# Spreading the scan decays of a state-space layer by one matmul of three rounded parts, and rounding the opening weight block earlier in the norms

## The reference

```
def _sublayer(x, fn, mod_j, g, b, weight):
    y = fn(x * (1 + scale) + shift)
    return _layernorm(DEEPNORM_ALPHA * x + weight * gate * y, g, b)

def step(state, inp):                     # the scan of the one state-space mixer
    acum = jnp.cumsum(dtc * a_g, axis=1)
    seg = acum[:, :, None] - acum[:, None, :]
    decay = jnp.exp(jnp.where(causal, seg, -jnp.inf))
    cb = jnp.einsum('blgn,bsgn->blsg', cc, bc)
    y = jnp.einsum('blsg,blsgh,bsghp->blghp', cb, decay, xc * dtc[..., None])
```

## Time and profile before

| | |
|---|---|
| time, median of 3 runs | 3048.01 us (3044.29 to 3054.64) |
| the profiled execution | 3059.89 us, its span 3058.1 us |
| PE busy | 91% of the span |
| DVE, ACT, POOL busy | 64%, 41%, 47% |
| granted TensorE clock, mean over the span | 0.918 |

### The profile page before, as it was taken

How to read it: one execution, slowest core, us unless ns; L and a number is a source line. 1 busy time by engine, 2 the same in 40 slices (tenths; PEclk the granted TensorE clock), 3 DMA queues, 4 the chain that set the end, 5 groups by cost and what they waited for, 6 DMA issues and landing times.

```text
span 3058.1 us, 49684 instructions
## 1 busy us (share of the span) xinstructions
PE 2769.6 (91%) x20691; PEld 2623.7 (86%) x20691; DVE 1963.1 (64%) x2277; ACT 1248.5 (41%) x1386; POOL 1449.5 (47%) x1134
## 2 busy tenths in 40 slices
PE   3998789999984999999989899999878999879999
PEld 3997689999983899999974899899768998679998
DVE  6656866576558765756676675765776555684654
ACT  2434444444433444444442443444434433344443
POOL 0890949659385396692970089298190000000000
PEclk7998889999996999999985899999889998889999
DMA  7775557667562576674740377486553643234453
GB/s 272 258 257 160 178 167 268 233 202 259 193 224 86 181 264 222 216 261 170 263 159 1 131 233 260 157 280 232 166 181 128 223 167 124 70 97 138 152 178 124
DMA packets 357446, 576.23 MB, mean 188 GB/s; under 512 B 22271, under 2 KB 297914, under 8 KB 357178
## 3 DMA queue, kind: packets, MB, share of 16 engines
q1 hardware_dynamic: 357306, 574.29, 55.6%
HBM read 573.20 MB, written 1.05 MB: 188 GB/s over the span
## 4 chain that ended last, share of the span: by engine, by line
PE 72%; DVE 12%; POOL 7%; ACT 3%; issue 3%; DMA 2%; SPq 1%; POOLq 0%; DVEq 0%; ACTq 0%
PE ps L1771 59%; POOL mod_acc L657 4%; PE ps L1824 3%; DVE wlo L1084 2%; POOL mod_w L652 2%; PE ps L2154 2%; ACT whi L695 1%; PE ps L1830 1%; PE ps L2145 1%; PE ps L1881 1%; DMA raw<-in_ffn_w_in_dram 1%; DVE z L1237 1%; DVE z L1215 1%; DMA mod_w<-in_w_mod_dram 1%; DVE conv L1514 1%
## 5 line engine op out<-in xcount | busy, mean ns | idle before, releaser
L1084 DVE TENSOR_TENSOR wlo<-raw,whi 128x2048 fp32r<-128x2048 f32 x387 | 982.4, 2541 | 620.7 <-ACT whi L695 618.9
L1771 PE MATMUL ps<-H_hi,whi 128*128 128x256 f32 x3840 | 1099.7, 286 | 47.1 <-issue 17.5
L1771 PE MATMUL ps<-H_lo,whi 128*128 128x256 f32 x3840 | 1093.5, 285 | 0.0
L1771 PE MATMUL ps<-H_hi,wlo 128*128 128x256 f32 x3840 | 1093.1, 285 | 0.0
L695 ACT ACTIVATE whi<-raw 128x2048 fp32r<-128x2048 f32 (+1 forms) x402 | 760.0, 1892 | 648.8 <-DMA raw<-in_ffn_w_in_dram 259.6
L1771 PEld LDWEIGHTS ps<-H_hi,whi 128*128 128x128 f32 x3840 | 744.3, 194 | 55.6 <-issue 45.8
L657 POOL TENSOR_TENSOR mod_acc<-mod_acc,mod_w 128x512 f32<-128x512 f32 x450 | 790.4, 1784 | 0.0
L1771 PEld LDWEIGHTS ps<-H_lo,whi 128*128 128x128 f32 x3840 | 744.5, 194 | 1.2 <-issue 1.0
L1771 PEld LDWEIGHTS ps<-H_hi,wlo 128*128 128x128 f32 x3840 | 744.2, 194 | 0.0
L1771 PE MATMUL ps<-A_hi,whi 128*128 (+1 forms) x1880 | 537.1, 286 | 21.5 <-DVE wlo L1084 21.5
L1771 PE MATMUL ps<-A_hi,wlo 128*128 (+1 forms) x1880 | 534.6, 284 | 0.0
(11 more groups left out here) (339 smaller groups left out, 2931.7 us busy)
## 6 DMA issues: line engine op xcount, KB each, us to landing
raw<-in_ffn_w_in_dram SPq DMA_DIRECT2D x176, 1024.0 KB, 5.3
mod_w<-in_w_mod_dram SPq DMA_DIRECT2D x180, 768.0 KB, 5.0
raw<-in_ffn_w_out_dram SPq DMA_DIRECT2D x88, 1024.0 KB, 5.0
raw<-in_w_gate_up_dram SPq DMA_DIRECT2D x22, 1024.0 KB, 5.1
raw<-in_ssm_w_in_dram SPq DMA_DIRECT2D x20, 1024.0 KB, 7.3
raw<-in_w_in_dram SPq DMA_DIRECT2D x14, 1024.0 KB, 5.1
raw<-in_diff_w_in_dram SPq DMA_DIRECT2D x12, 1024.0 KB, 8.1
raw<-in_w_down_dram SPq DMA_DIRECT2D x11, 1024.0 KB, 4.9
```

The source lines that it names most:

```text
L1084: tt(wlo[b % RAW][:, r], raw[b % RAW][:, r], whi[b % RAW][:, r].bitcast(F32), ALU.subtract).then_inc(w_lo, 1)
L1771: m = pe.matmul(out, l, r, start=first and i == 0, stop=last and i == 2, skip_group_check=rest)
```

## The change

Two edits. In the scan, the running sums are split into three parts (`ac_hi`, `ac_mid`, `ac_rest`), the three stand negated in 96 partitions of `acT` (now fp32r and 384 columns wide, with the second query half twice), and one fp32r matmul with `threefold` (three stacked unit matrices) adds them up again for head h. Ahead of it into the same bank goes an fp32r matmul of `mask` (1e30 above the diagonal) with `unit`, into the two diagonal blocks. ACT takes the exponential straight from that bank, with `dts[:, 7]` as bias and the scale -1, in two instructions. DVE's `decay` is gone. In the `ln` norms ACT rounds the second weight block before its square 2 and not before its square 4, and DVE takes its first half before `gated(2)` and not before `gated(4)`; `ln_last` stays as it was.

```
 # ACT, act_ln
-                    if c == 4:
+                    if c == (2 if st.kind == "ln" else 4):
                         convert(g.b + g.n + 1)
 # ACT, act_ssm
-                copy(acT[:, :], ps[0:SSM_H, 4, 0:S]).then_inc(s["acum_t"], 1)
+                copy(ac_hi[:, :], ps[0:3 * SSM_H, 4, 0:S]).then_inc(s["part_hi"], 1)
+                nc.scalar.activation(dts[:, 7], ps[:, 5, 0:64].rearrange("p (t h) -> p t h", t=2), ACT.Copy, scale=-1.0)
+                for i in range(3):
+                    r = slice(SSM_H * i, SSM_H * i + SSM_H)
+                    copy(threefold[r, :], ident[r, r])
+                act.wait_ge(s["rest_1"], n["rest_1"] + 1)
+                copy(ac_mid[:, :], ac_rest[:, :]).then_inc(s["part_mid"], 1)
...
+                act.wait_ge(s["rest_2"], n["rest_2"] + 1)
+                for i, x in enumerate((ac_hi[:, :].bitcast(F32), ac_mid[:, :].bitcast(F32), ac_rest[:, :])):
+                    r = slice(SSM_H * i, SSM_H * i + SSM_H)
+                    nc.scalar.activation(acT[r, 0:S], x[r, :], ACT.Copy, scale=-1.0)
+                    i = nc.scalar.activation(acT[r, S:CW], x[r, P:S], ACT.Copy, scale=-1.0)
+                i.then_inc(s["acum_t"], 1)
+                act.wait_ge(s["acum_t"], n["acum_t"] + 1)
                 for h in range(SSM_H):
-                    act.wait_ge(s["dec"], n["dec"] + h + 1)
-                    nc.scalar.activation(dec[:, h % 2, :], dec[:, h % 2, :], ACT.Exp).then_inc(s["dec_exp"], 1)
+                    act.wait_ge(s["spread"], n["spread"] + h + 1)
+                    if h >= 2:
+                        act.wait_ge(s["mixing"], n["mixing"] + h - 1)
+                    for t, (a, b) in enumerate(((0, S), (S, CW))):
+                        i = nc.scalar.activation(dec[:, h % 2, a:b], ps[:, 4 + h % 2, a:b], ACT.Exp, bias=dts[:, 7, t, h:h + 1], scale=-1.0)
+                    i.then_inc(s["dec_exp"], 1)
 # DVE, dve_ln
                 gated(0), gated(1), zsum(1), sqsum(1)
+                if st.kind == "ln":
+                    convert_open(st, 0)
                 gated(2), gated(3), zsum(2), zsum(3), sqsum(2), sqsum(3)
-                convert_open(st, 0)
+                if st.kind == "ln_last":
+                    convert_open(st, 0)
 # DVE, dve_ssm
+                dve.wait_ge(s["part_hi"], n["part_hi"] + 1)
+                tt(ac_rest[:, :], ps[0:3 * SSM_H, 4, 0:S], ac_hi[:, :].bitcast(F32), ALU.subtract).then_inc(s["rest_1"], 1)
...
+                tt(ac_rest[:, :], ac_rest[:, :], ac_mid[:, :].bitcast(F32), ALU.subtract).then_inc(s["rest_2"], 1)
...
-                    ts(dec[:, h % 2, 0:S], src, dts[:, 7, 0, h:h + 1], 0.0, ALU.subtract, ALU.min)
-                    ts(dec[:, h % 2, S:CW], src[:, P:S], dts[:, 7, 1, h:h + 1], 0.0, ALU.subtract, ALU.min).then_inc(s["dec"], 1)
 # PE, pe_ssm
                     if h >= 2:
-                        pe.wait_ge(s["dec"], n["dec"] + h - 1)
-                    pe.matmul(ps[:, 4 + h % 2, 0:S], ident[0:SSM_H, h:h + 1].to_broadcast([SSM_H, P]), acT[:, :], start=True, stop=True)\
+                        pe.wait_ge(s["dec_exp"], n["dec_exp"] + h - 1)
+                    to = ps[:, 4 + h % 2, 0:CW]
+                    pe.matmul(to.rearrange("p (j n) -> p j n", j=3)[:, 0:3:2, :], mask[:, :], unit[:, :].unsqueeze(1).to_broadcast([P, 2, P]),
+                              start=True, stop=False, skip_group_check=True)
+                    pe.matmul(to, threefold[:, h:h + 1].to_broadcast([3 * SSM_H, P]), acT[:, :], start=False, stop=True, skip_group_check=True)\
                         .then_inc(s["spread"], 1)
```

More of the change, by code:

```diff
@@ L172 @@
     "diff": dict(fin_sq=4, fin_sum=4, fin_std=4, fin_n=4, fin_hi=4, fin_lo=4, **{k: 8 for k in ATT}),
-    "ssm": dict(tap=24, conv_out=12, x_turned=8, x_out=8, dt_in=1, dt_ln=1, adt=1, acum=1, acum_t=1, cb=4, cb_out=4, spread=SSM_H,
-                dec=SSM_H, dec_exp=SSM_H, mixing=SSM_H, ssd=SSM_H, y_out=SSM_H // 2,
+    "ssm": dict(tap=24, conv_out=12, x_turned=8, x_out=8, dt_in=1, dt_ln=1, adt=1, acum=1, part_hi=1, rest_1=1, part_mid=1, rest_2=1, acum_t=1,
+                cb=4, cb_out=4, spread=SSM_H, dec_exp=SSM_H, mixing=SSM_H, ssd=SSM_H, y_out=SSM_H // 2,
                 fin_sq=4, fin_sum=4, fin_std=4, fin_n=4, fin_hi=4, fin_lo=4),
@@ L404, in program @@
         pick = at("pick", [P, 11], room(44), F32R)
+        unit, mask = at("unit", [P, P], room(4 * P), F32R), at("mask", [P, P], room(4 * P), F32R)
         std = at("std", [P, 2, S], room(8 * S))
@@ L451, in program @@
         dts = at("dts", [P, 8, 2, SSM_H], o_hf + 16 * S)
-        acT = at("acT", [SSM_H, S], o_hf + 16 * S + 4 * 512)
+        acT = at("acT", [3 * SSM_H, CW], o_hf + 16 * S + 4 * 512, F32R)
+        threefold = at("threefold", [3 * SSM_H, SSM_H], room(4 * SSM_H), F32R)
+        ac_hi, ac_rest = at("ac_hi", [3 * SSM_H, S], o_hl + 16 * CW, F32R), at("ac_rest", [3 * SSM_H, S], o_hl + 16 * CW + 4 * S)
+        a3 = at("a3", [P, 2, 3, SSM_H], o_hh + 16 * CW + 4 * S)
+        ac_mid = at("ac_mid", [3 * SSM_H, S], o_hh + 16 * CW, F32R)
         sqg = at("sqg", [P, 2, 4, S], o_hf)
@@ L766, in act_init @@
                 nc.scalar.activation(tiny[:, 6:8], tiny[:, 4:6], ACT.Exp).then_inc(s["lam_exp"], 1)
+                copy(unit[:, :], ident)
+                nc.scalar.activation(mask[:, :], kc("causal", 0, P), ACT.Copy, scale=-1.0)
                 copy(pick[:, :], kc("pick")).then_inc(s["picked"], 1)
@@ L963, in act_ssm @@
                 act.wait_ge(s["acum"], n["acum"] + 1)
-                copy(acT[:, :], ps[0:SSM_H, 4, 0:S]).then_inc(s["acum_t"], 1)
-                for h in range(SSM_H):
-                    act.wait_ge(s["dec"], n["dec"] + h + 1)
-                    nc.scalar.activation(dec[:, h % 2, :], dec[:, h % 2, :], ACT.Exp).then_inc(s["dec_exp"], 1)
+                copy(ac_hi[:, :], ps[0:3 * SSM_H, 4, 0:S]).then_inc(s["part_hi"], 1)
[5 more added lines that the diff above has]
+                copy(ac_mid[:, :], ac_rest[:, :]).then_inc(s["part_mid"], 1)
+                act.wait_ge(s["part_hi"], n["part_hi"] + 1)
+                act.wait_ge(s["part_mid"], n["part_mid"] + 1)
+                act.wait_ge(s["rest_2"], n["rest_2"] + 1)
[5 more added lines that the diff above has]
+                act.wait_ge(s["acum_t"], n["acum_t"] + 1)
+                for h in range(SSM_H):
+                    act.wait_ge(s["spread"], n["spread"] + h + 1)
[4 more added lines that the diff above has]
+                    i.then_inc(s["dec_exp"], 1)
                 act.wait_ge(s["y_out"], n["y_out"] + 16)
@@ L1531, in dve_ssm @@
                 link(tt(dts[:, 5], dts[:, 4], dts[:, 3], ALU.add))
-                stt(dts[:, 6], dts[:, 5], -1.0, alog[:, :].unsqueeze(1).to_broadcast([P, 2, SSM_H]), ALU.mult, ALU.mult).then_inc(s["adt"], 1)
-                dve.wait_ge(s["acum"], n["acum"] + 1)
-                link(nc.vector.tensor_copy(dts[:, 7], ps[:, 5, 0:64].rearrange("p (t h) -> p t h", t=2)))
+                for i in range(3):
+                    k = stt(a3[:, :, i, :], dts[:, 5], -1.0, alog[:, :].unsqueeze(1).to_broadcast([P, 2, SSM_H]), ALU.mult, ALU.mult)
+                k.then_inc(s["adt"], 1)
+                dve.wait_ge(s["part_hi"], n["part_hi"] + 1)
+                tt(ac_rest[:, :], ps[0:3 * SSM_H, 4, 0:S], ac_hi[:, :].bitcast(F32), ALU.subtract).then_inc(s["rest_1"], 1)
+                dve.wait_ge(s["rest_1"], n["rest_1"] + 1)
+                dve.wait_ge(s["part_mid"], n["part_mid"] + 1)
+                tt(ac_rest[:, :], ac_rest[:, :], ac_mid[:, :].bitcast(F32), ALU.subtract).then_inc(s["rest_2"], 1)
                 for i in range(SSM_G):
@@ L1563, in dve_ssm @@
                 for i in range(SSM_H + 3):
-                    if i < SSM_H:
-                        decay(i)
                     if 1 <= i <= SSM_H:
@@ L2127, in pe_ssm @@
                 pe.wait_ge(s["x_out"], n["x_out"] + 8)
[L2128 to L2131, removed]
+                a0, a1 = a3[:, 0, 0, :], a3[:, 1, 0, :]
+                a0s, a1s = (a3[:, t].rearrange("p c h -> p (c h)") for t in range(2))
+                of = ps[0:3 * SSM_H, 4, :]
+                pe.matmul(of[:, 0:P], a0s, tri, start=True, stop=True)
+                pe.matmul(of[:, P:S], a0s, ones, start=True, stop=False)
+                pe.matmul(of[:, P:S], a1s, tri, start=False, stop=True)
                 pe.matmul(ps[:, 5, 0:SSM_H], tri, a0, start=True, stop=True)
```

## The result

Before, the median was 3050.73 us over four runs (3044.29 to 3054.64), after it was 3008.93 us over four (3008.41 to 3013.01). The ratio is 0.9847, 95% interval 0.9827 to 0.9867. That is 41.8 us less between the medians, 41 to 53 by the interval. The profiled execution after took 3008.57 us, its span 3006.8 us; that is 51.3 us under the profiled one of before, which lay 9 us over its own median.

A forecast was written before the change was run, and what follows sets the result against it. PE paced the scan at 2.62 us a head at 1.2 GHz, hiding DVE's decay. Scan 38.2 - preparation 1.2 + norms 6.1 = 43.1 us off 3059.9 gives 3016.8; lowered to the runs' median, 3004.9 us, range 2995 to 3035.

The forecast's parts named there:

- The likeliest case: Scan: the granted clock rises from 0.50 to 1.00 and DVE paces the heads; 3004.9 us, chance 0.57.
- the rival of a low clock: Scan: clock stays at 1.2 GHz, 32 heads at 2.15 us, gain 14.7 us in all, 3033 us; chance 0.27.
- about three heads: Start of the scan: 3 heads at 1.2 GHz, 2.15 us each, before the clock rises.
- rows instead of gaps: Scan's clock: 32-row `spread` goes, leaving 128, 128 and 96 rows, which resembles the stretch before a rise.
- A head at 2.4 GHz: Scan, after the clock rises: DVE paces at 1.12 us, 1.17 with a hand-over; PE needs 1.08, ACT under 0.94.
- the bounds of 1.12 and 1.5: Scan, head at 2.4 GHz: from DVE's 1.12 us to 1.5 with PE and DVE taking turns in part.
- over 90%: Sign to look for in the profile after: DVE busy over 90% in the scan.
- 0.21 + 0.32 + 0.15 = 0.68 us: PE's `mask`, `acT` matmul and one gap per head at 1.2 GHz; with 1.47 for `mix`, 2.15 us a head.
- Halving it: Scan: at 2.4 GHz PE needs half of its 2.15 us at 1.2 GHz, 1.08 us a head.
- The scan's sum: 3 heads at 2.15, 29 at 1.17, 2.0 for the last: 42.4 us against 80.6, gain 38.2 us.
- The preparation: Ahead of the scan: splitting, queued `CB` products and uncovered table load delay the first `mixing`; cost 1.2 us, bounds 0 and 3.
- The norms: Earlier rounding gains 0.9 us in nine norms and loses 1.0 in two after latent attention: 6.1 us, bounds 0 and 9.

The follow-up runs named there:

- The edit alone: Only the scan's edit put into the kernel before, norms rounding the opening block as before: 3019.57 us, ratio 0.9886, 35.5 us less.

## Why the prediction was right, and where it was off

The forecast was 3004.9 us, 3008.9 came; the gain was put at 43.1 us and is 41.8 between the medians, 51.3 between the two profiled executions.

**The clock.** The likeliest case came, not the rival of a low clock: three heads at 0.50 and 1.00 from the fourth on, as "about three heads" said. The reason given, rows instead of gaps, is shown by the two kernels above: 32 rows to 128 raises it in the kernel before, 96 to 32 holds it down in the one after. That it took three heads was partly chance: other traces of the same scan had two to five.

**A head at 2.4 GHz.** The size was right and the pacer wrong. 1.17 us paced by DVE was predicted, 1.28 paced by PE measured, inside the bounds of 1.12 and 1.5; so DVE is busy 87% there and not over 90%. The failing term is "0.21 + 0.32 + 0.15 = 0.68 us", with one gap charged: at 1.2 GHz it measured 0.38 + 0.46 = 0.84, so each matmul leaves a gap, and the head takes 2.31 instead of 2.15. Halving it was the second error: 2.31 / 2 is 1.16, measured were 0.22 + 0.27 + 0.79 = 1.28. DVE would pace at about 1.10 us, as the kernel without mask shows, near the 1.12 of its sum; but no kernel here got PE below that: without the mask PE still takes 1.17.

**The scan's sum.** 44.2 us from the first `mixing` to the end of the last `output`, 42.4 predicted: a gain of 36.4 instead of 38.2. The edit alone gave 35.5 on the chip.

**The preparation.** 1.6 us lost, 1.2 predicted. Last was the fourth CB product, as forecast, and the table load behind the first `spread`. The prediction took the low clock of the first heads as given, because gaps were there before. Not seen was that it hangs on this preparation: with the gaps cut by the 2.1 us the clock stays up, which is worth another 1.3 to 4.3 us (43.1 to 46.1 against 41.7 us).

**The norms.** Predicted 9 x 0.9 - 2 x 1.0 = 6.1 us. PE's wait for the token sums fell from 1.57 to 0.67 us as in the sum, and the two norms after latent attention lost 0.82 and 0.81 us instead of 1.0. From the first `gated` to the token sums, all eleven together are 6.7 us shorter; that makes 0.9 us for each of the nine.

**Not counted, and there.** The group norms: from the last `output` to the projection 20.1 us before, 18.5 after, at a mean clock of 0.76 instead of 0.59. That makes 36.4 - 1.6 + 1.6 + 6.7 = 43.1 us in the trace, the predicted sum to the tenth, but by luck: scan, preparation, norms and group norms were off by -1.8, -0.4, +0.6 and +1.6 us.

**The other 8 us** between the two profiled executions lie in stretches that the change doesn't touch. The window of one of them, before:

```profile
827.00:1009.70 182.70, 130.20 (x851) 117.54 (x851) 130.25 (x183) 69.91 (x127) 110.54 (x106) 0.79 0.47 160
```

After:

```profile
822.60:1003.10 180.50, 127.19 (x851) 115.05 (x851) 129.46 (x184) 70.03 (x127) 109.97 (x106) 0.81 0.48 163
```

The same 851 matmul records take 3.0 us less of PE, at a slightly higher clock. Such stretches differ between any two traces here (this one took 180.5 to 185.4 us in five kernels that are alike in it), and the medians leave most of it out. Taking the sum from the slower profiled execution down to the median was right.

## What to carry to other kernels

Look at the granted clock and the rows of the array before counting what an engine does: a stretch in which PE is busy without a gap can still run at half speed, and then the work of every other engine in it looks hidden. Filling up the rows of a thin matmul with zeros cost nothing here and won 24.6 us by itself; try that before a redesign, and then see which engine paces. Ahead of a short stretch that depends on the clock, keep PE's waits short: another order of the preparation made it 2.1 us shorter, and the scan behind it took 41.7 us instead of 43.1 to 46.1. And an engine that looks close to full need not be the one that paces: DVE was busy 94% at 1.17 us a head, and PE set the time.

## What the runs showed of the hardware

- A 32-row fp32 matmul in 1.15 of 2.62 us held the clock at 1.2 GHz through 74 us of a busy PE; the same matmul in 128 rows held it at 2.4 GHz with PE busy 41.17 of 50.00 us.
- The first matmul of `spread` started together with its weight load and took some 0.1 us more to the next one: the spreading matmul of 384 columns took 0.37 to 0.38 us in that place and 0.27 behind the mask matmul.
- An fp32r matmul with output in two pieces of 128 columns took as long as one in a single piece, 0.22 us to the next one.
- Every ACT table load took 1.28 us (37 in each of the traces before and after), with at most 0.02 us to an instruction that was ready behind it. Moved into a wait of ACT it cost nothing: `ac_hi` follows the last XT copy by 1.64 us with it and without.
